# A 16-stage transformer kernel: one row shape for latent scores, GpSimd sums of squares, 258-token queries and a moved operand tile

## What is computed

```python
# latent layer: 16 heads, each 64 columns without and 32 with rotary positions; keys' rotary part is shared
k_nope, k_rope, v_shared = shared_latent_kv(h, kv_norm, kv_w_dkv, kv_a_norm, kv_w_ukv, pos)
h = mla_layer(h, b_attn_norm, b_w_dq, b_q_a_norm, b_w_uq, b_w_o, k_nope, k_rope, v_shared, ...)
# rms_norm: x * rsqrt(mean(x * x) + eps) * gain, before each matrix
# odd mixer: f_logit = proj[..., 3 * w:] + b_forget; log_f = log_sigmoid(f_logit)
return rms_norm(h, final_norm)[:, N_META:]
```

## Time and profile before

| | |
|---|---|
| three runs | 1228.75, 1229.19, 1229.86 us (median 1229.19) |
| the profiled execution | 1229.36 us, span 1227.6 us |
| mean granted TensorE clock | 0.998 of 2.4 GHz |
| PE busy | 1218.4 us (99%), 10067 matmul instructions |
| DVE, ACT, POOL busy | 887.1 (72%), 704.3 (57%), 160.5 us (13%) |

### The profile page before, as it was taken

The page is one execution under the profiler, slowest core; times in us unless marked ns, Lnnn a source line. Parts: engine busy times, 40 slices in busy tenths (PEclk is TensorE's granted clock), DMA queues, the critical chain, the costliest instruction groups (busy, mean ns, idle before and its releaser), DMA issues.

```text
span 1227.6 us, 26433 instructions
## 1 busy us (share of the span) xinstructions
PE 1218.4 (99%) x10067; PEld 1178.2 (96%) x10067; DVE 887.1 (72%) x1744; ACT 704.3 (57%) x1402; POOL 160.5 (13%) x166
## 2 busy tenths in 40 slices
PE   8999999999999999999999999999999999999998
PEld 8998999999997799999999899999999999999998
DVE  6988777776778977777678977766565877676543
ACT  6878555554465746555448865554345775555432
POOL 1111400002301040000562013000120002200000
PEclk9999999999999999999999999999999999999999
DMA  8333454534543135444467335555553333555551
GB/s 339 124 118 107 156 174 175 181 136 168 203 153 114 50 139 201 171 175 148 178 221 261 116 138 194 184 188 189 187 190 140 138 138 138 195 183 188 190 183 58
DMA packets 31711, 203.45 MB, mean 166 GB/s; under 512 B 3632, under 2 KB 4656, under 8 KB 11264
## 3 DMA queue, kind: packets, MB, share of 16 engines
...
q10 hardware_dynamic: 144, 0.28, 0.1%
...
## 4 chain that ended last, share of the span: by engine, by line
PE 92%; DVE 5%; ACT 1%; issue 1%; DMA 0%; SPq 0%; DVEq 0%; ACTq 0%
PE ps L746 27%; PE ps L747 27%; PE ps L748 27%; DVE w_lo L1876 1%; PE ps L1166 1%; PE ps L1132 1%; PE ps L841 1%; PE ps L1151 1%; PE ps L842 1%; PE ps L843 1%; PE ps L967 1%; PE ps L971 1%; PE ps L1008 1%; DVE E_S L2340 1%; PE ps L988 0%
## 5 line engine op out<-in xcount | busy, mean ns | idle before, releaser
L1876 DVE TENSOR_TENSOR w_lo<-raw,w_hi 128x1024 fp32r<-128x1024 f32 (+2 forms) x392 | 463.1, 1214 | 88.8 <-ACT w_hi L1367 87.9
L1367 ACT ACTIVATE w_hi<-raw 128x1024 fp32r<-128x1024 f32 (+2 forms) x392 | 377.1, 1002 | 184.4 <-PE ps L748 184.1
L746 PE MATMUL ps<-x_hi,w_hi 128*128 128x256 f32 (+2 forms) x1384 | 397.6, 287 | 2.5 <-issue 1.8
L747 PE MATMUL ps<-x_lo,w_hi 128*128 128x256 f32 (+2 forms) x1384 | 392.8, 284 | 0.0
L748 PE MATMUL ps<-x_hi,w_lo 128*128 128x256 f32 (+2 forms) x1384 | 392.3, 283 | 0.0
L746 PEld LDWEIGHTS ps<-x_hi,w_hi 128*128 128x128 f32 x1384 | 261.3, 189 | 4.6 <-issue 2.5
L747 PEld LDWEIGHTS ps<-x_lo,w_hi 128*128 128x128 f32 x1384 | 260.9, 189 | 0.5
L748 PEld LDWEIGHTS ps<-x_hi,w_lo 128*128 128x128 f32 x1384 | 261.0, 189 | 0.0
L746 PE MATMUL ps<-X_x_hi,w_hi 128*128 128x256 f32 (+2 forms) x568 | 162.5, 286 | 0.0
L748 PE MATMUL ps<-X_x_hi,w_lo 128*128 128x256 f32 (+2 forms) x568 | 161.2, 284 | 0.0
L747 PE MATMUL ps<-X_x_lo,w_hi 128*128 128x256 f32 (+2 forms) x568 | 160.8, 283 | 0.0
...
## 6 DMA issues: line engine op xcount, KB each, us to landing
...
```

The costliest lines, as they stand in the source:

```text
L746: pe.matmul(target, hi, xs[0], start=start, stop=False)
L747: pe.matmul(target, hi, xs[1], start=False, stop=False)
L1367: act.activation(w_hi[:, to + a:to + b], raw[:, fr + a:fr + b], ACT.Copy).then_inc(hi_made, 1)
L1876: dve.tensor_tensor(w_lo[:, to + a:to + b], raw[:, fr + a:fr + b], w_hi[:, to + a:to + b].bitcast(F32), ALU.subtract).then_inc(lo_made, 1)
```

## The change

1. **Latent scores.** GpSimd makes `krm`, two copies of the rotary key in which the 32 rows that do not belong to a head are zero. The rotary part then uses 64 rows per head, like the other part.
2. **Sums of squares of latents.** GpSimd adds the blocks, and PE multiplies one sum by ones instead of two and three blocks.
3. **258-token queries.** Blocks c2 to c4, n and r are made from token 14 on.
4. **Meta rows.** The 16-row operands `Vm` and `PTq` are read as 80 rows (the rest set to zero), and transposes of 16 rows take 128 or 80.
5. **Norm sums and gate.** For four norms GpSimd splits `acc` into fp32r parts, and PE makes two fp32r matmuls. The gate's weights' hi and lo stand side by side and are multiplied in one pass of 32 columns, with a second pass for the operand's rest.
6. **in1's operand** is written 6 columns later, so that the 256-token half begins at column 8.
7. **Places** of heads in stages A and B are moved.

```diff
-SCORES_AT = {"A": (5, 7, 9, 13, 15, 17, 21, 23), "B": (12, 14, 21, 23, 26, 28, 31, 32), ...
-TURN_AT = {"A": (7, 9, 11, 15, 17, 19, 23, 26), "B": (15, 19, 24, 27, 29, 31, 33, 35), ...
-MIX_AT = {"A": (8, 10, 12, 16, 18, 20, 25, 27), "B": (19, 21, 27, 29, 32, 33, 35, 36), ...
+SCORES_AT = {"A": (4, 7, 9, 13, 15, 17, 21, 23), "B": (12, 15, 21, 22, 26, 28, 30, 32), ...
+TURN_AT = {"A": (7, 9, 11, 15, 17, 19, 23, 26), "B": (15, 19, 25, 27, 29, 32, 34, 35), ...
+MIX_AT = {"A": (8, 10, 12, 16, 18, 20, 24, 28), "B": (19, 21, 27, 28, 32, 34, 35, 37), ...
...
-V_AT = (5, 6, 10, 12, 16, 18, 23, 25)
+V_AT = (3, 6, 10, 14, 16, 18, 22, 23)
 SUB_AT = (9, 11, 13, 17, 19, 21, 26, 28)
-OUT_AT = (10, 12, 14, 18, 20, 22, 27, 29)
+OUT_AT = (11, 11, 14, 19, 21, 25, 27, 29)
...
-        X["ffn1"] = raw_x("x2", "ffn1", 14, T - 14)
+        X["ffn1"] = raw_x("x2", "ffn1", 14, T - 14, at=6)
...
+        def key_rope(n, e, lo, cols):
+            return oB["krm"][64 * e:64 * e + 64, n % 2 * T + lo:n % 2 * T + lo + cols]
...
             def latent_sum(b, blocks):
-                pe.wait_ge(sq_made, blocks[-1] + 1)
+                pe.wait_ge(lat_added, 1 if blocks[0] == 0 else 3)
...
+                else:
+                    pe.wait_ge(krm_made, 4)
...
-                        p, r = rope_rows_of(n, e), n // 2 * T
-                        mm = pe.matmul(bank(3 + e, col, nk), oB["qr"][p, r + q0:r + q0 + P], oB["kr"][p, 0:nk],
-                                       start=False, stop=True, tile_position=(p.start, 0))
+                        p = slice(64 * e, 64 * e + 64)
+                        mm = pe.matmul(bank(3 + e, col, nk), oB["qr"][p, r + q0:r + q0 + P], key_rope(n, e, 0, nk),
+                                       start=False, stop=True)
...
-                        latent_sum(6, (0, 1))
+                        latent_sum(6, (0,))
...
-                        latent_sum(7, (2, 3, 4))
+                        latent_sum(7, (2,))
...
+                pe.matmul(bank(4, 0, n.n), ones_r[:, 0:1].broadcast_to([P, P]), acc_hi[:, 0:n.n], start=True, stop=False)
+                pe.matmul(bank(4, 0, n.n), ones_r[:, 0:1].broadcast_to([P, P]), acc_lo[:, 0:n.n], start=False, stop=True).then_inc(summed, 1)
...
+                    pe.matmul(bank(7, 0, SEQ, slice(0, 32)), oO["fgw"][:, at:at + 32], x[0], start=c == 0, stop=False)
+                    mm = pe.matmul(bank(7, 0, SEQ, slice(0, 16)), oO["fgw"][:, at:at + 16], x[1], start=False, stop=c == KC - 1)
...
-                pe.matmul(bank(7, 0, META), oA["Vm"][0:META, vc:vc + P], oA["PTq"][0:META, 32 * u:32 * u + META], start=True, stop=True)
+                pe.matmul(bank(7, 0, META), oA["Vm"][0:80, vc:vc + P], oA["PTq"][0:80, 32 * u:32 * u + META], start=True, stop=True)
...
+            def halves(n):
+                pool.wait_ge(ssq, n.ssq + n.chunks)
+                pool.tensor_copy(acc_hi[:, 0:n.n], acc[:, 0:n.n]).then_inc(halved, 1)
+                pool.wait_ge(halved, 2 * n.halved + 1)
+                pool.tensor_tensor(acc_lo[:, 0:n.n], acc[:, 0:n.n], acc_hi[:, 0:n.n].bitcast(F32), ALU.subtract).then_inc(halved, 1)
...
+            pool.wait_ge(done, ST["b_in"].turn)
+            pool.memset(oB["Vm"][0:80, :], 0.0).then_inc(vm_clear, 1)
+            pool.memset(oB["PTq"][0:80, :], 0.0).then_inc(vm_clear, 1)
+            for n, (m, c) in enumerate(((0, 1), (2, 3), (2, 4))):
+                lo = latent_first("c", m)
+                pool.wait_ge(sq_made, c + 1)
...
+                pool.tensor_tensor(to, to, oB["sq"][:, c * T + lo:c * T + T], ALU.add).then_inc(lat_added, 1)
+            pool.wait_ge(done, ST["b_in"].turn + 6)
+            pool.memset(oB["krm"][:, :], 0.0).then_inc(krm_clear, 1)
+            pool.wait_ge(krm_clear, 1)
+            pool.wait_ge(q_roped, 1)
+            for q in range(4):
+                rows = slice(32 * q, 32 * q + 32)
+                pool.tensor_copy(oB["krm"][rows, q % 2 * T:q % 2 * T + T], oB["kr"][rows, :]).then_inc(krm_made, 1)
```

More of the change, by code:

```diff
@@ L41 @@
 NEG = -1e30
-X2_AT = 20104
+X2_AT = 19600
 BIG = 3e38
@@ L425, in norm, with raw_x @@
             p.ssq, p.squared = take(ssq, chunks), take(squared, chunks - 1)
+            p.halved = take(halved, 1) if gain in IN_HALVES else None
             p.summed, p.lned, p.rstd = take(summed, 1), take(lned, 1), take(rstd_made, 1)
             return p
-        def raw_x(x, gain, first, n, among=1, nth=0, of=None):
+        def raw_x(x, gain, first, n, among=1, nth=0, of=None, at=0):
             p = Part()
+            p.at = at
             p.x, p.gain, p.first, p.n, p.among, p.nth = x, gain, first, n, among, nth
@@ L542, in program, with gate_weights @@
         ST["in0"].zeroed = take(dve_meta, 2)
+        def gate_weights(part):
+            return oO["fgw"][:, :].rearrange("p (c d k) -> p c d k", c=KC, d=2)[:, :, part, :]
         def unit_evicted(a, s):
@@ L905, in latent_block @@
                         x = c_tile(c + (2 if kind in ("n", "r") else 0))
-                    hi, lo = w_hi[:, at0 + w0:at0 + w0 + width], w_lo[:, at0 + w0:at0 + w0 + width]
+                    if lo:
+                        x = [v[:, lo:T] for v in x]
+                    w_parts = w_hi[:, at0 + w0:at0 + w0 + width], w_lo[:, at0 + w0:at0 + w0 + width]
                     if kind != "v":
@@ L917, in latent_block @@
                     to = bank(bank_of(st, s), 0, 512, rows)
-                    pe.matmul(to, x[0], hi, start=c == 0, stop=False)
-                    pe.matmul(to, x[0], lo, start=False, stop=False)
-                    mm = pe.matmul(to, x[1], hi, start=False, stop=c == kcs - 1)
+                    pe.matmul(to, x[0], w_parts[0], start=c == 0, stop=False)
+                    pe.matmul(to, x[0], w_parts[1], start=False, stop=False)
+                    mm = pe.matmul(to, x[1], w_parts[0], start=False, stop=c == kcs - 1)
                 if cs is None or kcs - 1 in cs:
@@ L924, in latent_sum @@
             def latent_sum(b, blocks):
-                pe.wait_ge(sq_made, blocks[-1] + 1)
+                pe.wait_ge(lat_added, 1 if blocks[0] == 0 else 3)
+                lo = latent_first("c", blocks[0])
                 for m in blocks:
-                    mm = pe.matmul(bank(b, 0, T), ones[:, :], oB["sq"][:, m * T:m * T + T], start=m == blocks[0], stop=m == blocks[-1])
+                    mm = pe.matmul(bank(b, lo, T - lo), ones[:, :], oB["sq"][:, m * T + lo:m * T + T], start=m == blocks[0], stop=m == blocks[-1])
                 mm.then_inc(f_summed, 1)
@@ L1002, in latent_mix @@
                     at = 32 * (n // 2) + 4 * (n % 2) + 2 * e
[L1003 to L1004 removed]
+                    pe.matmul(bank(7, 0, 2, slice(64 * e, 64 * e + 64)), oB["Vm"][0:80, vc + 64 * e:vc + 64 * e + 64],
+                              oB["PTq"][0:80, at:at + 2], start=True, stop=True)
                 for k, (lo, cols) in enumerate(((0, SEQ), (P, P))):
@@ L1171, in norm_sum @@
                 pe.wait_ge(ssq, n.ssq + n.chunks)
+                if n.halved is not None:
+                    pe.wait_ge(halved, 2 * n.halved + 2)
+                    pe.wait_ge(ones_rounded, 1)
                 if n.lned:
                     pe.wait_ge(lned, n.lned)
-                pe.matmul(bank(4, 0, n.n), ones[:, :], acc[:, 0:n.n], start=True, stop=True).then_inc(summed, 1)
+                if n.halved is None:
+                    pe.matmul(bank(4, 0, n.n), ones[:, :], acc[:, 0:n.n], start=True, stop=True).then_inc(summed, 1)
+                    return
+                pe.matmul(bank(4, 0, n.n), ones_r[:, 0:1].broadcast_to([P, P]), acc_hi[:, 0:n.n], start=True, stop=False)
+                pe.matmul(bank(4, 0, n.n), ones_r[:, 0:1].broadcast_to([P, P]), acc_lo[:, 0:n.n], start=False, stop=True).then_inc(summed, 1)
             def gain_sum():
@@ L1808, in lambdas @@
             def lambdas():
+                act.wait_ge(ones_set, 1)
+                act.activation(ones_r[:, :], ones[:, 0:8], ACT.Copy).then_inc(ones_rounded, 1)
                 act.wait_ge(dve_meta, 2)
@@ L2580, in squares @@
                     pool.tensor_tensor(acc[:, 0:n.n], acc[:, 0:n.n], sq[:, 0:n.n], ALU.add).then_inc(ssq, 1)
+                    if c == n.chunks - 1 and n.halved is not None:
+                        halves(n)
                     if with_gain:
```

155 lines of the change are left out of this document (90 added, 65 removed).

## The result

The changed kernel takes 1221.6 us (median of five executions) against 1229.19; the ratio is 0.9937, 95% interval [0.9925, 0.9949]. It is faster by 7.6 us, where 13.0 had been forecast; the time lies at the upper edge of the stated range, 1212.0 to 1221.5. Its profiled execution took 1221.97 us, span 1220.1.

A forecast was written before the change was run, and what follows sets the result against it. The prediction took PE's queue to bound the kernel (92% of the span), with DVE second. Terms saving 15.2 us less 2.2 us of new waits gave -13.0 us, 1216.2 us, range 1212.0 to 1221.5.

The forecast's parts named there:

- rival 2: Both head stages: DVE becomes the bound, half of what scores and mixes save becomes wait; 1220 us, 18%.
- Latent scores: Eight latent pairs: 0.66 us saved each with 64 rows throughout, 5.3 us in all (bounds 0 to 6.4).
- rival 1: Scores, mixes, transposes: new weights, not row shape, set the gap, so these save nothing; 1225 us, 7%.
- Mixes: Small matmuls at 80 rows: eight differential heads save 3.1 us, eight latent pairs 1.0 us.
- Norm sums: Four norms: two fp32r passes replace one fp32 sum, saving 0.8 us; GpSimd's new instructions lie beside blocks of passes.
- What is late next in B: Latent heads: new PE waits of 0.6 us at the first scores and 0.5 us between pairs.
- rival 4: Ahead of the first latent scores: GpSimd and DVE lock each other out, making it slower; 1230 to 1234 us, 3%.
- Stage A's waits: Stage A: PE waits some 0.6 us behind the last mix; 1.0 us taken for the whole stage.
- in1's tile: in1's 528 passes: the shifted start saves 2.2 ns each, 1.2 us in all (0 to 2.3, if both halves gain).
- rival 5: in1: the tile's shift does nothing, since columns alone set a pass's price; 1217.4 us, 10%.
- The small waits that I forecast: Stage A, first latent scores, between pairs, norm sums: new PE waits of 2.2 us together (0.5 to 6).
- Sums of latents, gate, transposes, 258-token queries: Four terms of PE's queue: savings of 1.4 us, 0.9 us, 0.7 us and 0.8 us, in that order.

The follow-up runs named there:

- e2: The changed kernel with the rotary half of the latent scores read from 32 rows again, GpSimd's key copies kept: 1225.0 us.
- e8: The changed kernel with the small matmuls of both kinds of mix read from 16 rows again instead of 80: 1223.15 us.
- e1: The changed kernel with the load of the forget gate's weights issued ahead of the last chunk's squares in front of mix1: 1218.36 us.
- e6: The changed kernel with all four norm sums as one fp32 instruction of PE again, without GpSimd's halves: 1218.79 us.
- e9: The changed kernel with the second and third part of the short value rows made by DVE instead of GpSimd: 1220.19 us.
- e4: The changed kernel with in1's gated tile beginning at column 0 of each chunk again, not at 6: 1223.34 us.
- e11: The changed kernel with all seven tables of places back at the values of the kernel before: 1225.49 us.
- e10: The changed kernel with 96 bytes of padding ahead of the stages' tiles, in1's tile staying where it is: 1221.46 us.

## Why the forecast was right and wrong

The direction and the main mechanism were right: the time falls mostly because row shapes no longer change (3.4 us by e2 and 1.5 by e8). The size was not: 7.6 us instead of 13.0. It lies at the upper edge of the range, which rival 2's 1220 us had widened; and part of what brought it there, the moved places, had hardly a term, so the range held it partly by luck.

- **Latent scores**: 5.3 forecast, 8 x 0.68 = 5.5 saved by the timeline; e2 confirms the cause and refutes rival 1. Only 3.4 of them reach the end, by e2.
- **Mixes**: the differential ones were mis-sized, 0.385 us each instead of 0.30 (2.4 instead of 3.1 us in all), since the 256-column matmul did not come down to its columns. Latent ones: 0.7 instead of 1.0.
- **Norm sums**: this is the step that failed. I wrote that GpSimd's two new instructions "lie beside two blocks of passes" and costed nothing. They were beside passes, but the load of the gate's weights is queued behind them, and PE asks for it. e1: 3.0 us. The gain itself was 0.4 instead of 0.8 (e6 against e1), since PE waits for the second half at one of the four.
- **What is late next in B**: I had 1.1 us. By the distances between starts PE stands 0.28, 1.70, 0.54, 0.62 and 0.22 us in the changed kernel (and 0.6 us at 378.8, as it did before). The largest is the lock: I had read its rows, and used them only for the new additions and copies (rival 4). The key copies end at 365.0 us, 0.3 us ahead of the rotated queries, so PE does not wait for them. Beside them three DVE instructions of the queries' rotation, each with two operands in SBUF, took 0.53, 0.63 and 0.52 us instead of 0.44, 0.43 and 0.44: the collision of rival 4 in its own place, worth 0.4 us of DVE, by the traces alone. The profile puts PE's 0.28 us ahead of the first scores down to ACT's L1619, which makes value rows. What I did not ask is what the collision of the earlier trace rows does once PE comes 4 us sooner. e9: 1.2 us.
- **Stage A's waits** were about right: 0.66 us behind the last mix against 0.6 forecast. The stretch gained 1.55 us, and 1.5 to 2.5 in the other runs, for 2.3.
- **in1's tile**: right in kind, and rival 5 is refuted by e4; both halves gained (my lower bound), 1.7 us instead of 1.2. By the rule of the Trainium skill, "TensorE: Matmul & The Clock Gate", section "Back-to-back issue gap", for a warm matmul by itself, the gap depends on columns alone. Four starts of the same 256 columns took 117.33 to 120.3 ns here at a granted clock of 1.00, so the measurement decides.
- **Places**: beyond the last mix of A (0.64 us gone, 0.6 come) I gave the moved tables no term. e11: 3.9 us. The small waits that I forecast presuppose them, which I had not seen.
- **Not foreseen**: the down stages lost 0.35 us each, because the added tensors moved their tile (e10), and out0 gained 0.7 us; why it did stays open.
- **Sums of latents, gate, transposes, 258-token queries**: no run isolates them. By the distances between starts in the two traces (the gate's in e1) the sums save PE 1.4 us, the gate 1.0 and the transposes 0.7, as forecast. Stage O without its wait gains 1.3 us for 1.4.

Rival 2 (1220 us) named a time nearer to the result than the forecast did, but not its cause: in stage B it was not DVE's load but one collision, since without it (e9), and with 1.9 us more work for DVE, 1.2 us come back at once; stage A was not tried. Rival 4 was the mechanism of that wait, at another place and at a tenth of its price.
